# One rotary-query chain for two heads, and key up-projections that share a weight block

## The reference

```python
q = q_cols.reshape(b, s, MLA_HEADS, QK_NOPE + QK_ROPE)              # 8 x (128 + 64)
q = jnp.concatenate([q[..., :QK_NOPE], rope(q[..., QK_NOPE:], pos)], axis=-1)
lat = rms_norm(ckv, kv_norm_g)
k_r = rope(kr[:, :, None, :], pos)[:, :, 0, :]                      # shared by the heads
lat_all = jnp.concatenate([cache_lat, lat], axis=1)
kv = jnp.einsum('blc,ce->ble', lat_all, w_ukv)                      # per head 128 k_nope + 128 v
k = jnp.concatenate([k_nope, jnp.broadcast_to(kr_all[:, :, None, :], ...)], axis=-1)
o = block_attention(q, k, v, pos, k_pos, True)
```

## Time and profile before

| | us |
|---|---|
| median of 3 runs | 4238.16 |
| lowest and highest of them | 4229.26, 4258.04 |
| span of the profiled execution | 4244.5 |
| PE busy in it | 3510.5 (83%) |
| DVE busy | 2838.9 (67%) |
| POOL busy | 1483.6 (35%) |
| ACT busy | 382.1 (9%) |

### The profile page before, as it was taken

How to read it: one execution, slowest core, us unless ns; L and a number is a source line. 1 busy time by engine, 2 the same in 40 slices (tenths; PEclk the granted TensorE clock), 3 DMA queues, 4 the chain that set the end, 5 groups by cost and what they waited for, 6 DMA issues and landing times.

```text
span 4244.5 us, 39396 instructions
## 1 busy us (share of the span) xinstructions
PE 3510.5 (83%) x14249; PEld 2510.1 (59%) x14249; DVE 2838.9 (67%) x3456; ACT 382.1 (9%) x954; POOL 1483.6 (35%) x1094
## 2 busy tenths in 40 slices
PE   7899999999999999999998689999979999970000
PEld 5465678887755555566766467777757777760000
DVE  5353442227677785676677878887885556569998
ACT  0311110000112110110000011000000000010000
POOL 0000000000015453453344443233443566577764
PEclk9999999999999999989999899999989999995555
DMA  8577555558449998998999997779999999999997
GB/s 335 197 277 285 199 197 185 194 194 298 162 186 377 376 381 350 380 370 361 420 417 412 410 351 309 299 301 379 417 405 372 410 404 405 407 353 407 410 400 320
DMA packets 251315, 1412.72 MB, mean 333 GB/s; under 512 B 35312, under 2 KB 83456, under 8 KB 86144
## 3 DMA queue, kind: packets, MB, share of 16 engines
q0 software_dynamic: 124704, 841.18, 49.0%
q1 hardware_dynamic: 68832, 501.25, 30.3%
q10 hardware_dynamic: 57632, 68.41, 4.5%
HBM read 1359.60 MB, written 51.16 MB: 332 GB/s over the span
## 4 chain that ended last, share of the span: by engine, by line
PE 48%; DMA 17%; DVE 17%; POOL 6%; issue 6%; DVEq 2%; PEld 2%; ACT 1%; PEldq 1%; ACTq 1%; POOLq 0%; SPq 0%
PE pq L401 47%; DMA first<-peer_v,experts 10%; DMA first<-peer_u,experts 6%; DVE pq L1705 5%; POOL first L1863 4%; DVE late L1705 3%; PEld pq L401 2%; DVE first L1695 2%; POOL got L1881 2%; DMA ring<-wstream 2%; PE pq L405 1%; ACT arena L798 1%; POOL ring L1863 1%; ACTq L812 1%; DVE arena L1478 1%
## 5 line engine op out<-in xcount | busy, mean ns | idle before, releaser
L401 PE MATMUL pq<-h_last,ring 128*128 128x288 f32 (+2 forms) x6688 | 1704.7, 414 | 84.0 <-issue 56.3
L401 PEld LDWEIGHTS pq<-h_last,ring 128*128 128x128 f32 (+2 forms) x6688 | 1258.1, 191 | 524.0 <-issue 142.3
L1863 POOL DMA_INDIRECT first<-peer_u,experts x256 | 419.7, 1639 | 1746.2 <-DVEq L1540 1243.4
L1863 POOL DMA_INDIRECT first<-peer_v,experts x464 | 660.7, 1424 | 843.5 <-DVEq L1706 752.2
L401 PE MATMUL pq<-first,ring 128*128 128x256 f32 (+2 forms) x3104 | 703.4, 386 | 21.0 <-issue 8.9
L1705 DVE SCALAR_TENSOR_TENSOR late<-first,wts,late 128x2048 f32<-128x2048 f32 x254 | 597.3, 2352 | 177.6 <-DMA first<-peer_v,experts 163.7
L1695 DVE CUSTOM_DVE_ANT_0 first<-first,late 128x2048 f32<-128x2048 f32 x256 | 582.3, 2291 | 197.9 <-DMA first<-peer_u,experts 189.8
L401 PEld LDWEIGHTS pq<-first,ring 128*128 128x128 f32 (+2 forms) x3104 | 575.2, 188 | 142.8 <-issue 43.3
L1705 DVE SCALAR_TENSOR_TENSOR pq<-first,wts,pq 128x2048 f32<-128x2048 f32 x142 | 334.5, 2355 | 112.4 <-DMA first<-peer_v,experts 102.8
L1881 POOL DMA_INDIRECT got<-dots_dram,at_dot x288 | 322.9, 1121 | 104.2 <-issue 91.1
L401 PE MATMUL pq<-arena,ring 128*128 128x256 f32 (+2 forms) x1216 | 301.0, 405 | 48.0 <-DVEq L1447 32.4
(11 more groups left out here) (197 smaller groups left out, 2009.4 us busy)
## 6 DMA issues: line engine op xcount, KB each, us to landing
ring<-wstream SPq DMA_DIRECT2D x478, 1024.0 KB, 7.5
dots_dram<-wts ACTq DMA_DIRECT2D x8, 2304.0 KB, 8.1
dots_dram<-stage ACTq DMA_DIRECT2D x128, 144.0 KB
first<-peer_v,experts POOLq DMA_INDIRECT x464, 11.3
got<-dots_dram,at_dot POOLq DMA_INDIRECT x288
first<-peer_u,experts POOLq DMA_INDIRECT x256, 10.1
out<-arena ACTq DMA_DIRECT2D x6, 512.0 KB, 6.4
o_last<-x_t ACTq DMA_DIRECT2D x5, 576.0 KB, 16.9
```

The lines of the kernel that those rows point to most:

```text
L401: return nc.tensor.matmul(out, lhsT, rhs, start=start, stop=stop)
L1863: g.indirect_dma_start(out=slots[slot], out_offset=None, in_=peer_u if kind == "u" else peer_v, in_offset=bass.IndirectOffsetOnAxis(ap=exp ...
```

## The change

Two heads share a chain. The rotary weights of heads h and h+1 (h even) fill one block of 2048 columns, and one chain with 128 output rows gives both heads' rotary queries; it runs in the even head, and is evicted, rotated and kept on 128 partitions. The scores of the odd head read partitions 64 to 127, for which the rotary key is held twice. The key up-projections of the pair share a second block, 1024 columns wide, which the even head reads first and the odd head releases. In odd heads the q block now stands ahead of the modulation blocks. Blocks that are used in part are loaded as wide as used (1024 for kn, 1152 for the block `krf`).

```diff
     for _h in range(NH):
+        if _h % 2 == 1:
+            place(_g, "q", _h, B_MLA + 4 * _h + 2)
         if _g == 0:
             place(0, "mod", 2 * KC + 2 * _h, B_MLA + 4 * _h)
             place(0, "mod", 2 * KC + 2 * _h + 1, B_MLA + 4 * _h + 1)
-        place(_g, "q", _h, B_MLA + 4 * _h + 2)
-        place(_g, "rkn", _h, B_MLA + 4 * _h + 3)
+        if _h % 2 == 0:
+            place(_g, "q", _h, B_MLA + 4 * _h + 2)
+            place(_g, "r", _h // 2, B_MLA + 4 * _h + 3)
+            place(_g, "kn", _h // 2, B_MLA + 4 * _h + 7)
         unit(_g, "q", _h)
-        unit(_g, "r", _h)
+        if _h % 2 == 0:
+            unit(_g, "r", _h // 2)
...
+WIDE = {B_KRF: KC * (ROPE + NH)}
+WIDE.update({B_MLA + 4 * _h + 3: 2 * 4 * HD for _h in range(1, NH, 2)})
...
-                sp.dma_start(ring[:, n % RING, :], wstream[b]).then_inc(w_in[n % RING], 16)
+                w = WIDE.get(b, D)
+                sp.dma_start(ring[:, n % RING, 0:w], wstream[b, :, 0:w]).then_inc(w_in[n % RING], 16)
...
-                s = block_at((g, "rkn", i))
-                project((g, "r", i), s, 0, ROPE, hg[g])
+                if i % 2 == 0:
+                    s = block_at((g, "r", i // 2))
+                    project((g, "r", i // 2), s, 0, 2 * ROPE, hg[g])
+                    pe.drain().then_inc(w_used[s], 1)
+                s = block_at((g, "kn", i // 2))
                 for c, keys_of in enumerate([latT[:, :, 0:WG[0]]] if g == 0 else [latT[:, :, 0:KHALF], latT[:, :, KHALF:NKEY]]):
-                    project((g, "kn", i, c), s, KC * ROPE, P, keys_of)
-                pe.drain().then_inc(w_used[s], 1)
+                    project((g, "kn", i, c), s, (i % 2) * 4 * HD, P, keys_of)
+                if i % 2 == 1:
+                    pe.drain().then_inc(w_used[s], 1)
...
-                    last = mm(ps, qr[:, q], krT[:, ks], False, True)
+                    last = mm(ps, qr[half, q], krT[half, ks], False, True)
...
-                             (krT[:, T:NKEY], kr_cache)):
+                             (krT[0:ROPE, T:NKEY], kr_cache), (krT[ROPE:, T:NKEY], kr_cache)):
...
-                a(rope_x[:, 0:w], ps[0:ROPE, 0:w])
-                a(rope_r[0:32, 0:w], ps[32:64, 0:w])
-                a(rope_r[32:64, 0:w], ps[0:32, 0:w])
+                a(rope_x[0:heads * ROPE, 0:w], ps[0:heads * ROPE, 0:w])
+                for o in range(0, heads * ROPE, ROPE):
+                    a(rope_r[o:o + 32, 0:w], ps[o + 32:o + 64, 0:w])
+                    a(rope_r[o + 32:o + 64, 0:w], ps[o:o + 32, 0:w])
...
-                v.tensor_tensor(dst, rope_x[:, 0:w], rope_r[:, 0:w], ALU.add)
+                for dst in dsts:
+                    v.tensor_tensor(dst, rope_x[0:m, 0:w], rope_r[0:m, 0:w], ALU.add)
...
-                    rotate(qr[:, 0:WG[g]], g, 9 * g + i + 2)
+                    if i % 2 == 0:
+                        rotate([qr[:, 0:WG[g]]], g, RT * g + i // 2 + 2, 2 * ROPE)
```

More of the change, by code:

```diff
@@ L347, in build @@
         block = ctx.enter_context(nc.Block())
-        NSMALL = 7
+        NSMALL = 8
+        RT = 1 + NH // 2
         def later(i):
@@ L518, in latents @@
                 mla_values(g, 0)
-                pe.wait_ge(rope_ok, 9 * g + 1)
+                pe.wait_ge(rope_ok, RT * g + 1)
                 pe.wait_ge(f_z, g + 1)
                 for i, t in enumerate(GT[g]):
-                    last = tr(pb[7][0:rows(t), i * ROPE:(i + 1) * ROPE], krT[:, t * P:t * P + rows(t)])
+                    last = tr(pb[7][0:rows(t), i * ROPE:(i + 1) * ROPE], krT[0:ROPE, t * P:t * P + rows(t)])
                 last.then_inc(krt_ps, 1)
@@ L542, in scores_mla @@
             def scores_mla(g, h):
-                pe.wait_ge(rope_ok, 9 * g + h + 2)
-                evicted((g, "r", h))
+                pe.wait_ge(rope_ok, RT * g + h // 2 + 2)
+                evicted((g, "r", h // 2))
+                half = slice((h % 2) * ROPE, (h % 2 + 1) * ROPE)
                 evicted((g, "kn", h, 0))
@@ L858, in keep_unit, with keep_rope @@
                 a(dst, pb[unit_bank(key)][0:m, 0:w], **kw).then_inc(proj_free[unit_bank(key)], 1)
-            def keep_rope(key, n, w):
+            def keep_rope(key, n, w, heads):
                 act.wait_ge(proj, unit_done(key))
@@ L892, in latents @@
                 act.drain().then_inc(lat_ss, 1)
-                ps = keep_rope((g, "krf"), 9 * g, w)
+                ps = keep_rope((g, "krf"), RT * g, w, 1)
                 a(fT[:, 0:w], ps[ROPE:ROPE + NH, 0:w]).then_inc(proj_free[unit_bank((g, "krf"))], 1)
@@ L960, in evict_mla @@
                 keep_unit((g, "q", i), qn[:, 0:w], P, w)
-                keep_rope((g, "r", i), 9 * g + 1 + i, w)
-                act.drain().then_inc(proj_free[unit_bank((g, "r", i))], 1)
-                act.drain().then_inc(rope_in, 1)
+                if i % 2 == 0:
+                    keep_rope((g, "r", i // 2), RT * g + 1 + i // 2, w, 2)
+                    act.drain().then_inc(proj_free[unit_bank((g, "r", i // 2))], 1)
+                    act.drain().then_inc(rope_in, 1)
                 for c in range(g + 1):
@@ L1342, in latents @@
                 dve.drain().then_inc(lat_rs, 1)
-                rotate(krT[:, CG[g]:CG[g + 1]], g, 9 * g + 1)
+                rotate([krT[o:o + ROPE, CG[g]:CG[g + 1]] for o in (0, ROPE)], g, RT * g + 1, ROPE)
                 dve.wait_ge(f_ps, g + 1)
@@ L1969 @@
         put(block(w_in[:, h * q_w:h * q_w + HD]))
-        put(pad(block(w_in[:, h * q_w + HD:(h + 1) * q_w]), block(ukv_h[:, h, 0])))
+        if h % 2 == 0:
+            put(block(np.concatenate([w_in[:, i * q_w + HD:(i + 1) * q_w] for i in (h, h + 1)], axis=1)))
+        else:
+            put(pad(block(ukv_h[:, h - 1, 0]), block(ukv_h[:, h, 0])))
     for c in range(2):
```

19 lines of the change are left out of this document (10 added, 9 removed).

## The result

The changed kernel takes 4255.95 us in the median (4250.65 to 4265.11), the kernel before 4240.78 in the runs beside it (4225.58 to 4258.04). The ratio is 1.0032, with a 95% interval of 1.0023 to 1.0042: some 14 us slower. The forecast was 4237, one microsecond faster than the median then shown. The time lies in the forecast range; the change of the time does not go the way forecast.

What follows compares the result with a forecast made beforehand. PE was taken to bound pass 0 MLA, gathers and DVE pass 1 with PE close behind. Pass 0 +3.9 and pass 1 -4.7 gave -0.8 us, median 4238.16 to 4237; range 4208 to 4258, core 4222 to 4252 (0.65).

Steps and rivals of the forecast that it cites:

- Chains and small edits of pass 0: Pass 0 MLA: a pair takes 34.4 us instead of 41.1, four save 26.8; small edits cost 1.1.
- The ring in pass 0: Pass 0: PE waits for q behind the shared kn block's release before heads 2, 4, 6; 21.3 us in sum.
- The clock: Pass 0: the chain behind each of three ring stalls runs slower, 2.75 us each, 8.3 in all.
- Pass 0 in sum: Pass 0 MLA: -26.8 chains, +21.3 ring, +8.3 clock, +1.1 small edits, giving +3.9 us.
- the rival of stalls that cost more than the chains give: Pass 0: even heads start late and at the lower clock; +20.6 us there, 4260 with nothing won in pass 1; chance 0.13.
- What the rival of a ring that keeps up promised: Pass 0: loads land in time or stalls cost no clock, -7 to -26 us; kernel 4203 to 4226; chance 0.17.
- Pass 1: Pass 1 MLA: -5.8 us from fewer ring bytes, +1.1 for small edits, giving -4.7.
- DVE itself loses four rotations: Pass 1: DVE is spared four rotations of 1.53 us, 6.1 in all.
- The ring brings 2 MiB less ... I take half: Pass 1: fewer ring bytes, 5.5 us; half of the -11.6 bound with DVE's rotations is taken, -5.8.
- gathers and DVE set that stretch, and PE follows closely: Pass 1 MLA: DVE waits 45.1 us for gathered rows, 3.6 for PE's scores; PE waits 5.96 for DVE in head 7.
- A shared kn block makes no stall here: Pass 1: without modulation blocks, the next even q block takes a slot released a whole pair earlier; no stall.
- The signs named for the two passes: Pass 0: ring waits about 6, 6, 9 us, clock near 0.5; pass 1: PE's waits for DVE from 9 to some 30.

Runs made afterwards that it cites:

- e1: Changed kernel, pass 0 only: even heads load q ahead of modulation blocks, odd heads chain kn before q; 4233.11 us, ratio 0.9962 to the kernel before.
- e3: Pass 0 as in the changed kernel, pass 1 as in the kernel before; 4249.88 us, ratio 1.0014 to the kernel before.
- e2: Pass 0 as in the kernel before, pass 1 as in the changed kernel; 4254.19 us, ratio 1.0021 to the kernel before.
- e10: Kernel before, but in pass 1 SP holds each head's q load until the previous head's rotary chain has ended; 4257.54 us, ratio 1.0034.
- e15: e6, but in pass 1 DVE rotates the next even head's queries three rows of experts sooner; 4222.87 us, ratio 0.9951 to the kernel before.
- e11: e6, but SP holds four loads of pass 1 for events of PE; 4221.51 us, ratio 0.9946 to the kernel before.
- e13: e11, but q of head 6 is held for an event some 20 us sooner; 4224.80 us, ratio 0.9956 to the kernel before.
- e14: e8, but SP holds 14 loads of pass 1 each for a given gathered row; 4254.18 us, ratio 1.0026 to the kernel before.
- e6: e1, with odd heads chaining kn before q in pass 1 too; 4224.49 us, ratio 0.9962 to the kernel before.
- e5: Pass 0 as in e1, pass 1 as in the kernel before; 4217.30 us, ratio 0.9946 to the kernel before.
- e8: Kernel before, but odd heads of pass 1 omit their rotary chain, eviction and rotation, with blocks and loads unchanged; 4249.13 us, ratio 1.0017.
- e12: e5 without the kn-first order in odd heads of pass 0, q still loaded first in even heads; 4222.22 us, ratio 0.9951 to the kernel before.

## Why the prediction was wrong

**Chains and small edits of pass 0**: right. A pair was put at 34.4 us, e1 has 34.9, 1.2 of it a wait for the ring. The 1.1 of small edits is not shown: the first q chain starts 1.3 later than before, but over the runs it starts between 195.31 (e3, same pass 0) and 199.38 (e2).

**The ring in pass 0**: right in mechanism, place and size. Forecast 6.2, 6.2 and 8.9; measured 7.09, 7.25 and 8.64, sum 23.0 against 21.3. By the Trainium skill's "DMA: Bandwidth & Descriptors", "Anatomy of one DMA", the estimated stalls were 3 us shorter in sum, about 18; the rows do not agree with it. That section gives its figures for transfers that GpSimd issues, which the prediction does not say; SP issues these.

**The clock**: right. 2.75 each; measured 10.07 - 7.17 = 2.9, 3.0 and 1.9. The granted 0.53 behind the first wait agrees with the "HAM oscillation" section of "TensorE: Matmul & The Clock Gate" in the Trainium skill.

**Pass 0 in sum**: +3.9 forecast, +4.6 in the trace (3.3 of it from the first q chain on), 1.0014 in e3. Stall and lost clock are 10.0, 10.3 and 10.5 us at the three boundaries, in sum 30.8 against the 29.6 forecast. So the rival of stalls that cost more than the chains give, with its whole chains at half clock, did not come: by the medians pass 0 makes the smaller part of the loss, 6 of 15 us, though the intervals of e2 and e3 overlap. What the rival of a ring that keeps up promised, e1 delivers once the loads are put in order.

**Pass 1**: wrong, and with it the sign. The term was -4.7, with the step "DVE itself loses four rotations" and "The ring brings 2 MiB less ... I take half"; its bounds went from -11.6 to nothing, and the half was a guess between them. e2 measures +9 us, outside them. Two things were missed. First, I wrote that "gathers and DVE set that stretch, and PE follows closely", from 5.96 and 45.1 us of waits in one execution; four other executions of the unpaired form have a stage of 226.5 to 229.9 us, in three of them with PE at a clock of 1.00 and DVE waiting 26 to 28 us. There PE sets the pace, with the transfers at 0.99 just behind it: its chains release the slots and so space the loads. In the execution that I read the stage took 234.1 us, and why is open. Second, I counted the bytes that the ring brings, not when. "A shared kn block makes no stall here" was true of PE and beside the point: the held block, its followers on SP's queue and PE's new wait for the rotation turned loads every 13 and 16 us into 0.4, 16, 8 and 40, and DVE then waited for late rows. That bunches cost is shown by e10. That PE's wait for the rotation makes most of it in the changed kernel is suggested by the stage of e15, not shown in the time. The signs named for the two passes did appear: DVE's waits for gathers no smaller, PE's for DVE up to 18.2 + 14.2.

**The range**: that the time lies in it is luck. Its slow end came from longer stalls and a lower clock in pass 0 with nothing won in pass 1; a loss in pass 1 was in no bound and no rival. Also, I wrote that a measurement cannot tell about 1% from no change; with 20 runs on each side the interval is 0.1% to either side.

**Open**: how much of pass 1's loss is bunching and how much the lower clock behind PE's waits. Holding loads (e11, e13, e14) brought part or none of it back, and e15 changed both at once (the clock of its stage is 0.93 against 0.90 in e6).

## What to carry to other kernels

In an in-order ring, a block shared by two consumers holds its slot for both and everything behind it on the queue: put the load that is needed first, not a filler, on that slot, and run the last reader of the shared block early. Before work is taken from an engine that is not the only bound, ask what it paces: here PE's even chains spaced the transfers that the gathers had to live beside. Read a stage from several executions before a bound is named, and look whether the profiled one is near the median.

## What was not expected of the hardware

A delay of loads alone, with every engine's work as before, made a stage of 226.5 to 234.1 us one of 251.0 and the kernel some 14 us slower (e10). With PE's busy time in that stage down from 219.8 us (e5) to 202.8 (e2, with 2 MiB less to load) or 203.3 (e8, with the same loads), it took 237.7 and 239.9 us. In e12 a q chain took 8.86 us instead of 7.17 behind a wait of 1.11, at a granted clock of 0.81; in e2 the q chain of head 1 in pass 0 took the same 8.86, at the same 0.81, with no wait right ahead of it (0.87 for the rotation 2 us earlier), and behind the same 0.87 the kernel before took 7.17. So that loss need not come from the wait.
